# Mixture-of-experts layer on one core: from one 64-row expert block per pass to two blocks per pass, one in each column group of TensorE

## Chip, core and metric

One NeuronCore of a Trainium2 chip runs the whole layer in float32. The time is the device time of one execution in microseconds; the median of a few executions is given. The compute engines are PE (TensorE), DVE (VectorE), ACT (ScalarE), POOL (GpSimd) and SP (SyncE, which only issues DMAs here); 16 DMA engines move data.

## What is computed

A layer over 512 latent tokens of width 1024 with 256 context tokens: a projection, differential attention with four heads beside a pooling group, an output projection, and then a mixture of 64 SwiGLU experts (8 per token) with one shared expert. All that the change touches is the mixture:

```python
scores = jax.nn.sigmoid(t @ w_router)            # 512 x 64, top 8 per token in 4 of 8 groups
...
def expert_block(args):
    tok, wb, e = args
    xb = t_pad[tok]
    yb = swiglu(xb, w_e_gate[e], w_e_up[e], w_e_down[e])   # 1024 -> 256 -> 1024
    return yb * wb[:, None]
...
routed = jax.ops.segment_sum(yb.reshape(P, d), slot_tok, num_segments=T + 1)[:T]
shared = swiglu(t, w_sh_gate, w_sh_up, w_sh_down)
```

Every expert's weights are 3 MB (gate, up and down of 1 MB each), 201 MB in all, and each is read once. The 4096 pairs of token and expert are sorted by expert and cut into blocks of 64 slots; an expert with no full block has one part-filled block, and each has at least one.

## The kernel before

The first half (projections, attention, output projection, up to about 330 us) is not touched, but for where its results are kept. Each engine runs its own program, written out by hand, and they meet at semaphores.

**Routing and slot table (330 to 390 us).** DVE finds each token's eight experts, and from ranks (`ranks`, PE) the block and the place of every selected pair. The table of slots (which token and weight stands in each place of each block) is a product of one-hot matrices: `onehots(c)` on DVE makes the block one-hots (128 blocks wide, once with the token number, once with the weight), `pick_rows(c)` on ACT makes the place one-hots with eight Abs and one Relu, and `slot_table(c)` on PE multiplies them, 256 columns wide, for four chunks of 128 tokens. `quarters` (PE) spreads token numbers over partitions for the gather indices. Between these, PE does the shared expert (`shared_gate_up`, `shared_hidden`, `shared_down`), whose rows ACT stores to `sums[0]`. DVE writes `tab` (the expert of each block) and `ltab` (for each expert, the count of `s_dn` at which its last block is done).

**Weight stream (SP).** `wring` holds six experts. `load(n)` issues three 1 MB DMAs for expert n-1 (n = 0 is the shared expert). Before each, SP waits for `arrived(n-2)`, so that two are in flight, and then for `s_dn` to reach `ltab` of the expert whose slot is taken (lines 470 to 478, DMA issue at L432, arrival at L436).

**The expert loop.** A pass handles one block of 64 rows. PE's array is used as two column groups of 64 columns. Both work on the same block: group 0 takes the first half of the expert's columns straight from `wring`, group 1 the second half from a copy, `cur_g` (gate and up, made by DVE, two buffers, L1559) or `cur_d` (down, made by ACT, L761). Pass b on PE is: transpose of the hidden rows of block b-1 (`turn_hidden`, L1157), gate and up of block b (`gate_up`, L1141), down of block b-1 (`down`, L1150). The loop body is written for two passes (q = 0, 1) and the buffers alternate. In each pass:
- DVE (L1573 to L1582): waits for the next block's weights and copies half of gate and up; waits for the next block's gathered rows and transposes them (`turn_block`, L1563); multiplies silu, up and the slot weights (`hmid`, L1578); keeps the transposed hidden rows (L1582).
- ACT (L828 to L835): silu (L830), the index of a later gather (L765), the copy of half of the down weights (L761), then `keep_y`: when the scatter two passes back has landed, it copies the down product to `ysb` (L824), and the scatter's index (L768).
- POOL (L558, L559): two indirect gathers (L521) of 1 KB quarter rows of `h_rows` for block b+3, into `xg`, and one indirect scatter (L528) that adds 2 KB half rows to `sums[q]` in memory. Even and odd blocks add to different buffers, so two scatters may be in flight.

**Tail.** When all scatters have landed, SP and ACT load both sums, DVE adds and normalises them, and the output is stored; rows of the first two tiles are added to `out` by an accumulating DMA.

Of the kernel before, what the change touches and what calls it, by code (L numbers as in the profile page):

```python
# [23 lines left out]
P = 128  # L24
D = 1024
# [21 lines left out]
MAXB = 128  # L47
CW = KD * F
# [26 lines left out]
def constants():  # L75
# [16 lines left out]
    for a in range(NT):  # L92
        c[:, C_TOK + a] = 2 * (a * P + p) - FAR
    c[:, C_U] = p
    c[:, C_HALF] = FAR + p // SUB
    c[:, C_LO:C_LO + P] = (p % SUB + 1)[None]
# [7 lines left out]
    c[:, C_QUART] = 2 * FAR + p // 32  # L104
# [3 lines left out]
def build(nc, a, hbuf, sums, out):  # L108
    with ExitStack() as ctx:
# [14 lines left out]
        slot_idx = sb("slot_idx", [P, 136], I32)  # L124
        gidx = sb("gidx", [P, 2, 2], I32)
        sidx = sb("sidx", [P, 2], I32)
        slot_w = sb("slot_w", [P, 136])
        xg = sb("xg", [P, 2, D // 2])
# [13 lines left out]
        with ExitStack() as second:  # L142

            def sb2(name, shape, dt=F32):
                return second.enter_context(nc.sbuf_tensor(name, shape, dt))

            wring = sb2("wring", [P, NB * EW])
            cur_g = sb2("cur_g", [P, 2, 2, KD, P])
            cur_d = sb2("cur_d", [P, FJ, D // 2])
# [67 lines left out]
        nslo = kept[:, 832:864]  # L217
        pick = [heads[:, 3072 * i:3072 * i + 1024].rearrange("p (k q) -> p k q", k=TOPK) for i in range(2)]
        place2 = [heads[:, 3072 * i + 1024:3072 * i + 3072].rearrange("p (k v b) -> p k v b", k=TOPK, v=2)
# [3 lines left out]
        slot_g = cst[:, C_TRI:C_TRI + 2 * 136].bitcast(I32)  # L223
        vraw = rows[:, 1024:1024 + MAXB]
        xT = rows[:, 0:1024].rearrange("p (b k q) -> p b k q", b=2, k=KD)
        ysb = rows[:, 1024:2048].rearrange("p (b n) -> p b n", b=2)
        ysh = [hTt[i].rearrange("p k t -> p (k t)") for i in range(NT - 1)]
        ysh.append(cur_d[:].rearrange("p j n -> p (j n)"))
# [3 lines left out]
        sg = rows[:, 2048:2176]  # L232
        hmid = rows[:, 2304:2432]
        hTb = rows[:, 2560:2816].rearrange("p (b q) -> p b q", b=2)

# [96 lines left out]
        s_slo = sem("places_in_block")  # L332
        s_pick = sem("place_onehots")
# [13 lines left out]
        s_gt = [sem(f"gathered{i}") for i in range(2)]  # L347
        s_xte = sem("block_transposed")
# [9 lines left out]
        s_scat = [sem(f"scattered{i}") for i in range(2)]  # L358
# [6 lines left out]
        s_mixed = [sem(f"mixed_rows_stored{i}") for i in range(ADDED)]  # L365
# [18 lines left out]
        def _(sp):  # L384
# [33 lines left out]
            def load(n):  # L418
                if n == 0:
                    srcs = (a["w_sh_gate"][0].rearrange("(p k) f -> p (k f)", k=KD),  # L420
                            a["w_sh_up"][0].rearrange("(p k) f -> p (k f)", k=KD),
                            a["w_sh_down"][0].rearrange("(j p) n -> p j n", j=FJ))
                else:
                    srcs = (a["w_e_gate"][0, n - 1].rearrange("(p k) f -> p (k f)", k=KD),
                            a["w_e_up"][0, n - 1].rearrange("(p k) f -> p (k f)", k=KD),
                            a["w_e_down"][0, n - 1].rearrange("(j p) n -> p j n", j=FJ))
                for s, src in enumerate(srcs):
                    o = (n % NB) * EW + s * CW
                    dst = wring[:, o:o + CW]
                    if s == 2:  # L430
                        dst = dst.rearrange("p (j n) -> p j n", j=FJ)
                    sp.dma_start(dst, src).then_inc(s_wl[n % NB], 16)  # L432
# [6 lines left out]
            sp.dma_start(sums[1].rearrange("(p r) (h n) -> p (r h) n", p=P, h=2),  # L439
# [8 lines left out]
            for t in range(NT):  # L448
                if t < ADDED:
                    sp.wait_ge(s_x1, t + 1)  # L450
                    sp.dma_start(out[0, t * P:(t + 1) * P, :], xres[:, t, :]).then_inc(s_mixed[t], 16)
# [18 lines left out]
            for n in range(NB, NE):  # L470
# [3 lines left out]
                else:  # L474
                    if n == NB + 1:
                        sp.wait_ge(s_tab, 1)
                    sp.wait_ge(s_dn, sp.value_load(ltab[0:1, n - NB - 1:n - NB], min_val=NT + 2, max_val=MAXB + NT + 1))
                load(n)
            for n in range(NE - 2, NE):
                arrived(n)  # L480

            sp.wait_ge(s_routed, 1)
            for t in range(NT):
                sp.dma_start(acc[:, 0, t, :], sums[0][t * P:(t + 1) * P, :]).then_inc(s_yin[t][0], 16)
# [7 lines left out]
        def _(pool):  # L492
# [22 lines left out]
            srows = [x.rearrange("t (h n) -> (t h) n", h=2) for x in sums]  # L515

            def gather(b, q, set_by):
                pool.wait_ge(s_gi, set_by)
                pool.sem_inc(s_pgo, 1)
                for s in range(2):  # L520
# [1109 lines left out]
```

## Time and profile before

| | before |
|---|---|
| median of 3 runs | 1053.07 us (1050.58 to 1053.62) |
| profiled execution | 1052.63 us |
| its span | 1050.8 us |
| mean granted TensorE clock | 0.976 |
| PE busy | 963.3 us (92%) |
| DVE busy | 544.2 us (52%) |
| ACT busy | 377.6 us (36%) |
| POOL busy | 507.8 us (48%) |
| DMA | 296.18 MB, mean 282 GB/s |

The span runs from the first to the last instruction of the profiled execution, the time beside it is that of the same execution seen from outside. A busy share is a mean over stages with different limits. The page of the profile has the busy times, the span in 40 slices, the queues, the chain of work that ended last, and the costliest groups of instructions; views of the trace give the same for a stretch, an engine or a line. A float32 matmul stands in the trace as two records. Row costs on the DMA queues are told here as engine-us per MB: the share of the 16 engines, times the length of the stretch, times 16, by the MB moved. q1 is SP's queue, q10 ACT's and q0 POOL's.

### The profile page before, as it was taken

How to read it: one execution, taken by the hardware profiler on the slowest of the kernel's cores; microseconds unless marked ns; L12 is line 12 of the kernel's file. 1: busy time of each engine (PE TensorE's matmuls, PEld its weight loads, DVE VectorE, ACT ScalarE, POOL GpSimd, SP SyncE). 2: the span in 40 equal slices, each digit the busy share in tenths (PEclk: the TensorE clock that was granted, in tenths of full speed). 3: DMA queues.
4: the chain of work that ended last, by engine and by line, in shares of the span. 5: the costliest groups of instructions: out<-in, count | busy, mean ns of one | idle time of the engine just before them, and what ended most of it. 6: DMA issues, size and time to landing. Idle time of an engine off the chain costs nothing.

```text
span 1050.8 us, 19751 instructions
## 1 busy us (share of the span) xinstructions
PE 963.3 (92%) x5619; PEld 507.9 (48%) x5620; DVE 544.2 (52%) x833; ACT 377.6 (36%) x822; POOL 507.8 (48%) x351
## 2 busy tenths in 40 slices
PE   3999999899999998989999987999899999999970
PEld 0554444466555554545555444555455555555530
DVE  2336786777166834544555353455355545545434
ACT  4212222377245442323333333333233433333322
POOL 0312431000000025857777665777577777777751
PEclk9999999999999999999999999999999999999995
DMA  9955452800011958999998999999999999999917
GB/s 369 345 177 200 166 209 85 332 2 1 1 80 63 415 211 314 391 393 382 364 362 284 398 396 377 376 368 353 377 375 358 363 365 307 389 374 357 333 23 240
DMA packets 78313, 296.18 MB, mean 282 GB/s; under 512 B 18421, under 2 KB 19137, under 8 KB 58577
## 3 DMA queue, kind: packets, MB, share of 16 engines
q1 hardware_dynamic: 49874, 255.92, 62.1%
q0 software_dynamic: 26416, 35.70, 14.8%
q10 hardware_dynamic: 2000, 4.28, 1.0%
q8 instruction: 11, 0.18, 0.1%
q14 instruction: 12, 0.10, 0.0%
HBM read 280.83 MB, written 37.49 MB: 303 GB/s over the span
## 4 chain that ended last, share of the span: by engine, by line
PE 49%; DMA 36%; issue 5%; DVE 3%; SPq 2%; POOL 2%; ACT 2%; POOLq 0%; ACTq 0%; DVEq 0%
DMA wring<-in_w_e_down 29%; PE psum L905 13%; PE psum L1141 11%; PE psum L1150 5%; DMA xg<-h_rows,gidx 3%; PE psum L995 3%; PE psum L1107 3%; PE psum L975 3%; PE psum L942 3%; PE psum L966 2%; DMA ring<-in_w_ada 2%; POOL xg L521 1%; SPq L432 1%; DMA expert_sums<-rows,sidx 1%; PE psum L1084 1%
## 5 line engine op out<-in xcount | busy, mean ns | idle before, releaser
L1141 PE MATMUL psum<-wring,rows 128*64 x1664 | 389.3, 388 | 0.6
L1141 PE MATMUL psum<-cur_g,rows 128*64 128x256 f32 x1664 | 389.5, 389 | 0.0
L521 POOL DMA_INDIRECT xg<-h_rows,gidx x214 | 275.5, 1287 | 177.6 <-issue 106.8
L1141 PEld LDWEIGHTS psum<-wring,rows 128*64 128x64 f32 x1664 | 223.2, 139 | 122.8 <-issue 12.4
L1141 PEld LDWEIGHTS psum<-cur_g,rows 128*64 128x64 f32 x1664 | 223.6, 139 | 0.0
L1559 DVE COPY cur_g<-wring 128x2048 f32 x105 | 131.1, 1248 | 148.7 <-issue 75.3
L1150 PE MATMUL psum<-wring,rows 128*64 x420 | 197.5, 593 | 4.4 <-ACT cur_d L761 2.3
L528 POOL DMA_INDIRECT expert_sums<-rows,sidx x107 | 177.9, 1663 | 43.0 <-issue 32.1
L1150 PE MATMUL psum<-cur_d,rows 128*64 128x512 f32 x420 | 197.5, 593 | 0.0
L1563 DVE STREAM_TRANSPOSE rows<-xg 128x512 f32<-128x512 f32 x105 | 116.3, 1108 | 65.1 <-DMA xg<-h_rows,gidx 64.9
L761 ACT COPY cur_d<-wring 128x1024 f32 x104 | 108.9, 1047 | 99.1 <-PE psum L1150 88.5
L905 PE MATMUL psum<-actT,ring 128*128 128x512 f32 (+1 forms) x256 | 98.1, 547 | 1.3 <-DVE actT L1250 1.3
L830 ACT ACTIVATE rows<-psum 128x128 f32<-128x128 f32 x104 | 28.8, 277 | 192.0 <-PE psum L1141 192.0
L1150 PEld LDWEIGHTS psum<-wring,rows 128*64 128x64 f32 x420 | 57.4, 137 | 79.4 <-issue 64.7
L537 POOL TENSOR_TENSOR heads<-heads 128x512 f32<-128x512 f32 x4 | 5.1, 1270 | 162.0 <-DVE heads L1377 162.0
L1582 DVE COPY rows<-psum 128x128 f32<-128x128 f32 x104 | 30.4, 292 | 93.5 <-PE psum L1157 91.1
L510 POOL TENSOR_TENSOR ring<-ring 128x2048 f32<-128x2048 f32 x8 | 36.4, 4556 | 77.4 <-ACT ring L628 77.4
L905 PEld LDWEIGHTS psum<-actT,ring 128*128 128x128 f32 x256 | 49.8, 195 | 49.0 <-issue 46.9
L1157 PEld LDWEIGHTS psum<-cst,rows 128*128 128x128 f32 x105 | 14.7, 140 | 113.9 <-DVE rows L1578 112.3
L824 ACT COPY rows<-psum 128x512 f32<-128x512 f32 x105 | 61.1, 582 | 23.0 <-DMA expert_sums<-rows,sidx 19.9
L1157 PE MATMUL psum<-cst,rows 128*128 128x128 f32 x105 | 34.9, 333 | 27.7 <-DVE rows L1578 27.4
L1150 PEld LDWEIGHTS psum<-cur_d,rows 128*64 128x64 f32 x420 | 57.5, 137 | 0.0
(227 smaller groups left out, 937.0 us busy)
## 6 DMA issues: line engine op xcount, KB each, us to landing
wring<-in_w_e_gate SPq DMA_DIRECT2D x64, 1024.0 KB, 8.8
wring<-in_w_e_up SPq DMA_DIRECT2D x64, 1024.0 KB, 12.0
wring<-in_w_e_down SPq DMA_DIRECT2D x64, 1024.0 KB, 18.4
ring<-in_w_ada SPq DMA_DIRECT2D x20, 1024.0 KB, 4.9
ring<-in_w_in SPq DMA_DIRECT2D x4, 2048.0 KB, 29.2
heads<-in_w_ada SPq DMA_DIRECT2D x4, 1024.0 KB, 23.1
ring<-in_w_out SPq DMA_DIRECT2D x1, 4096.0 KB, 15.2
xg<-h_rows,gidx POOLq DMA_INDIRECT x214
```

Source lines behind the costliest of these rows:

```text
L510: pool.tensor_tensor(part[:, 2048:], part[:, 2048:], wrow[1], ALU.add).then_inc(s_part[1], 1)
L521: pool.indirect_dma_start(xg[:, q, 256 * s:256 * s + 256], None, hrows, bass.IndirectOffsetOnAxis(gidx[:, q, s:s + 1].bitcast(U32), 0), bo ...
L528: pool.indirect_dma_start(srows[q], bass.IndirectOffsetOnAxis(sidx[:, q:q + 1].bitcast(U32), 0), ysb[:, q, :], None, bounds_check=2 * T - ...
L761: act.copy(cur_d[:], w[:, :, D // 2:]).then_inc(s_cdn, 1)
L824: act.copy(ysb[:, q, :], pp[0][:, 512 * q:512 * q + 512]).then_inc(s_yev, 1)
L905: last = pe.matmul(o, l, r, start=(k == 0), stop=(k == KD - 1))
L942: last = pe.matmul(psum[:, o0:o0 + n], qT[64 * s:64 * s + 64, h, t * P:(t + 1) * P], kT[64 * s:64 * s + 64, h, c0:c0 + n], start=True, sto ...
L1141: last = pe.matmul(pp[2][SUB * g:SUB * g + SUB, 512 * q:512 * q + 2 * P] .rearrange("p (u f) -> p u f", u=2), xT[:, q, k, :], cur_g[:, q, ...
L1150: last = pe.matmul(pp[0][SUB * g:SUB * g + SUB, 512 * q:512 * q + 512], hTb[:, q, SUB * j:SUB * j + SUB], cur_d[:, j, :] if g else wring[: ...
L1157: pe.transpose(pp[3][:, 512 * q:512 * q + P], hmid, ident).then_inc(s_ht, 1)
L1559: dve.tensor_copy(cur_g[:, q], w[:, :, :, P:]).then_inc(s_cgu, 1)
L1563: dve.transpose(xT[:, q].rearrange("p k (s r) -> p s k r", s=2), xg[:, q, :].rearrange("p (s r k) -> p s k r", s=2, k=KD)).then_inc(s_xte, 1)
```

## The change

- A pass handles a pair of blocks, 2p and 2p+1. Column group 0 takes the first with all 256 (1024) columns of its expert from `wring`; group 1 the second with all columns of its expert from `cur_g` and `cur_d`, which now hold a whole expert each, in one buffer. `tab` is read for both blocks.
- `cur_g` is copied in two parts (3 and 5 of the 8 k), after the pair before has finished its gate and up; DVE's order in a pass becomes transpose, hidden product, copy, hidden rows. `cur_d` is copied in two parts (j).
- A gather fetches the pair's 128 rows with four indirect DMAs of 1 KB quarter rows, for pair p+2; a scatter adds 128 whole rows of 4 KB. Both halves add into one tensor of 1024 rows (group 0 into the first 512, group 1 into the others); each scatter's rows are kept only after the scatter before it has landed.
- `ltab` counts pairs.
- `w_e_down` is read with rows 2p and 2p+1 on partition p, 8 KB in one piece, and the hidden columns are transposed with a step of 2 to fit.
- The slot table is 128 places by 64 pairs; DVE makes the place one-hots with one compare, and `pick_rows` on ACT is gone.
- The buffers move: `xT` and `ysb` into `xres`, whose rows are therefore stored to `out` for all four tiles and the last two read back (`x1b`) at the end.

```diff
+PAIRS = MAXB // 2
+FIRST_KS = 3
...
-    c[:, C_HALF] = FAR + p // SUB
-    c[:, C_LO:C_LO + P] = (p % SUB + 1)[None]
+    c[:, C_HALF] = FAR + p // SUB * T
+    c[:, C_LO:C_LO + P] = (p + 1)[None]
...
-                            a["w_e_down"][0, n - 1].rearrange("(j p) n -> p j n", j=FJ))
+                            a["w_e_down"][0, n - 1].rearrange("(p j) n -> p (j n)", j=FJ))
...
+            sp.wait_ge(s_dn, sp.value_load(ltab[0:1, NE - NB - 1:NE - NB], min_val=NT + 2, max_val=PAIRS + NT + 1))
+            for t in range(ADDED, NT):
+                sp.wait_ge(s_mixed[t], 16)
+                sp.dma_start(x1b[:, t, :], out[0, t * P:(t + 1) * P, :]).then_inc(s_x1b, 16)
...
-            with pool.Fori(0, nb, 2) as i:
+            pairs = pool.snap((nb + 1) // 2)
+            with pool.Fori(0, pairs, 2) as i:
                 for q in range(2):
-                    gather(i + (q + 3), 1 - q, i + (q + 3))
-                    scatter(i + (q - 1), 1 - q)
+                    gather(i + (q + 2), q, i + (q + 2))
+                    scatter(i + (q - 1), 1 - q, ysb[:, 1 - q], i + (q + 2))
...
             def copy_down(e, w0):
                 act.wait_ge(s_w, e + 2)
-                w = wring[:, bass.ds(w0, CW)].rearrange("p (j n) -> p j n", j=FJ)
-                act.wait_ge(s_sh_st[NT - 1], 16)
-                act.copy(cur_d[:], w[:, :, D // 2:]).then_inc(s_cdn, 1)
+                for j in range(FJ):
+                    act.copy(cur_d[:, j, :], wring[:, bass.ds(w0 + j * D, D)]).then_inc(s_cdn, 1)
...
             def keep_y(n, q, scattered):
                 act.wait_ge(s_dn, n)
-                act.wait_ge(s_scat[q], scattered)
-                act.copy(ysb[:, q, :], pp[0][:, 512 * q:512 * q + 512]).then_inc(s_yev, 1)
-
-            with act.Fori(0, nb, 2) as i:
+                act.wait_ge(s_scat, scattered)
+                act.copy(ysb[:, q], pp[q]).then_inc(s_yev, 1)
+
+            with act.Fori(0, pairs, 2) as i:
                 for q in range(2):
+                    gather_index(i + (q + 2), q)
                     e, w0 = down_weights(i + q)
                     act.wait_ge(s_gu, i + (q + NT + 1))
-                    act.activation(sg, pp[2][:, 512 * q:512 * q + P], ACT.Silu).then_inc(s_sil, 1)
-                    gather_index(i + (q + 3), 1 - q)
+                    act.activation(sg, pp[2][:, 512 * q:512 * q + F], ACT.Silu).then_inc(s_sil, 1)
                     act.wait_ge(s_dn, i + (q + NT + 1))
                     copy_down(e, w0)
-                    keep_y(i + (q + NT + 1), 1 - q, i * 8 + 16)
+                    keep_y(i + (q + NT + 1), 1 - q, i * 16 + (16 * q + 16))
                     scatter_index(i + (q - 1), 1 - q)
...
-            def gate_up(q, w0):
+            def gate_up(p, q, w0):
                 w = wring[:, bass.ds(w0, 2 * CW)].rearrange("p (u k f) -> p u k f", u=2, k=KD)
+                pe.wait_ge(s_cgu, p * 2 + 1)
                 for k in range(KD):
+                    if k == FIRST_KS:
+                        pe.wait_ge(s_cgu, p * 2 + 2)
                     for g in range(2):
-                        last = pe.matmul(pp[2][SUB * g:SUB * g + SUB, 512 * q:512 * q + 2 * P]
+                        last = pe.matmul(pp[2][SUB * g:SUB * g + SUB, 512 * q:512 * q + 2 * F]
                                          .rearrange("p (u f) -> p u f", u=2),
-                                         xT[:, q, k, :], cur_g[:, q, :, k, :] if g else w[:, :, k, 0:P],
+                                         xT[:, q, k, SUB * g:SUB * g + SUB], cur_g[:, :, k, :] if g else w[:, :, k, :],
                                          start=(k == 0), stop=(k == KD - 1))
                 last.then_inc(s_gu, 1)
...
-            def down(q, w0):
+            def down(copied, q, w0):
                 for j in range(FJ):
-                    for g in range(2):
-                        last = pe.matmul(pp[0][SUB * g:SUB * g + SUB, 512 * q:512 * q + 512],
-                                         hTb[:, q, SUB * j:SUB * j + SUB],
-                                         cur_d[:, j, :] if g else wring[:, bass.ds(w0 + (2 * CW + j * D), 512)],
-                                         start=(j == 0), stop=(j == FJ - 1))
+                    pe.wait_ge(s_cdn, copied + j)
+                    for m in range(2):
+                        for g in range(2):
+                            last = pe.matmul(pp[q][SUB * g:SUB * g + SUB, 512 * m:512 * m + 512],
+                                             hTb[:, j, SUB * g:SUB * g + SUB],
+                                             cur_d[:, j, 512 * m:512 * m + 512] if g else
+                                             wring[:, bass.ds(w0 + (2 * CW + j * D + 512 * m), 512)],
+                                             start=(j == 0), stop=(j == FJ - 1))
                 last.then_inc(s_dn, 1)
...
-                then(dve.tensor_tensor(b[:, :, 1, :], row(C_IOTA, MAXB), col(sblk, MAXB), ALU.is_equal))
+                dve.tensor_tensor(pick[c % 2], row(C_LO, P), col(slo, P), ALU.is_equal)
+                then(dve.tensor_tensor(b[:, :, 1, :], row(C_IOTA, PAIRS), col(sblk, PAIRS), ALU.is_equal))
...
-            with dve.Fori(0, nb, 2) as i:
+            pairs = dve.snap((nb + 1) // 2)
+            with dve.Fori(0, pairs, 2) as i:
                 for q in range(2):
                     e, w0 = gate_up_weights(i + (q + 1))
-                    dve.wait_ge(s_gu, i + (q + NT))
-                    copy_gate_up(e, w0, 1 - q)
-                    turn_block(1 - q, i * 16 + 32 * (q + 1))
+                    turn_block(1 - q, i * 32 + 64 * (q + 1))
                     dve.wait_ge(s_sil, i + (q + NT + 1))
                     dve.scalar_tensor_tensor(hmid, sg, slot_w[:, bass.ds(i + q, 1)],
-                                             pp[2][:, 512 * q + P:512 * q + 2 * P], ALU.mult, ALU.mult)\
+                                             pp[2][:, 512 * q + F:512 * q + 2 * F], ALU.mult, ALU.mult)\
                        .then_inc(s_hm, 1)
+                    dve.wait_ge(s_gu, i + (q + NT + 1))
+                    copy_gate_up(e, w0)
                     dve.wait_ge(s_ht, i + (q + NT + 2))
-                    dve.tensor_copy(hTb[:, q, :], pp[3][:, 512 * q:512 * q + P]).then_inc(s_hte, 1)
+                    dve.wait_ge(s_dn, i + (q + NT + 1))
+                    dve.tensor_copy(hTb, pp[3][:, 512 * q:512 * q + F].rearrange("p (j q) -> p j q", j=FJ))\
+                       .then_inc(s_hte, 1)
```

## Rows read from the trace of the kernel before

**Rows 1.** The page: items of the chain that ended last; costliest group.
```profile
DMA wring<-in_w_e_down 29%; PE psum L905 13%; PE psum L1141 11%; PE psum L1150 5%; DMA xg<-h_rows,gidx 3%; PE psum L995 3%; PE psum L1107 3%; PE psum L975 3%; PE psum L942 3%; PE psum L966 2%; DMA ring<-in_w_ada 2%; POOL xg L521 1%; SPq L432 1%; DMA expert_sums<-rows,sidx 1%; PE psum L1084 1%
...
L1141 PE MATMUL psum<-wring,rows 128*64 x1664 | 389.3, 388 | 0.6
```

**Rows 2.** Busy time by stretch: PE, PEld, DVE, ACT, POOL, granted clock, DMA share, GB/s.
```profile
525.00:550.00 25.00, 25.00 (x190) 13.51 (x192) 13.05 (x18) 10.25 (x23) 19.57 (x14) 1.00 1.04 365
550.00:575.00 25.00, 25.00 (x183) 12.69 (x177) 13.10 (x18) 8.93 (x22) 18.88 (x14) 1.00 0.87 273
```

**Rows 3.** SyncE's waits, 460 to 1000 us: releaser: us in total, times, longest.
```profile
SPq L436 <- DMA wring<-in_w_e_down: 413.0, 51, 9.9
SPq L432 <- PE psum L1150: 20.9, 4, 8.8
```

**Rows 4.** DMA queues, 460 to 1000 us: packets, MB, share of 16 engines.
```profile
q1 hardware_dynamic: 29363, 164.70, 76.6%
q0 software_dynamic: 22034, 31.14, 24.6%
```

**Rows 5.** Chain in order of time: start us, us, what.
```profile
480.25 3.67 PE psum L1141 x32
...
558.44 3.60 PE psum L1141 x32
562.04 1.72 PE psum L1150 x8
563.76 0.26 PE psum L1157
...
772.09 9.25 DMA expert_sums<-rows,sidx
...
810.05 8.18 DMA xg<-h_rows,gidx
```

**Rows 6.** SyncE in order of time: loads 7, 22, 43 and 54 begin.
```profile
409.59 0.34 SPq L432 DMA_DIRECT2D wring<-in_w_e_gate  x1
...
563.80 0.33 SPq L432 DMA_DIRECT2D wring<-in_w_e_gate  x1
...
760.41 0.33 SPq L432 DMA_DIRECT2D wring<-in_w_e_gate  x1
...
882.15 0.33 SPq L432 DMA_DIRECT2D wring<-in_w_e_gate  x1
```

**Rows 7.** DMA queue q1, 3 to 22 us (w_ada, rows of 8 KB).
```profile
q1 hardware_dynamic: 1408, 7.71, 99.5%
```

**Rows 8.** DMA queue q1, 199 to 203 us (w_out, rows of 4 KB).
```profile
q1 hardware_dynamic: 222, 1.58, 99.1%
```

**Rows 9.** DMA queue q0, 1042 to 1050 us (accumulating stores, rows of 4 KB).
```profile
q0 software_dynamic: 195, 0.67, 46.6%
```

**Rows 10.** The page: groups of instructions, busy us, mean ns, idle before.
```profile
L521 POOL DMA_INDIRECT xg<-h_rows,gidx x214 | 275.5, 1287 | 177.6 <-issue 106.8
...
L528 POOL DMA_INDIRECT expert_sums<-rows,sidx x107 | 177.9, 1663 | 43.0 <-issue 32.1
...
L761 ACT COPY cur_d<-wring 128x1024 f32 x104 | 108.9, 1047 | 99.1 <-PE psum L1150 88.5
```

**Rows 11.** Scatters (tile expert_sums): time from issue to landing.
```profile
DMA to landing us min/median/max: 3.5/8.5/19.6
```

**Rows 12.** PE in order of time, slot table chunks 2 and 3.
```profile
369.56 7.49 PE L1084 MATMUL psum<-heads 128*128 128x256 f32 x32 [1.03 <-ACT heads L750]
```

**Rows 13.** DVE in order of time: the last useful copy of gate and up weights.
```profile
1002.91 1.23 DVE L1559 COPY cur_g<-wring 128x2048 f32 x1 [6.31 <-SPq L436]
```

**Rows 14.** Chain in order of time, last passes.
```profile
1005.78 5.36 PE psum L1141 x32
...
1020.81 1.96 PE psum L1150 x8
```

**Rows 15.** DMA queue q0, 550 to 575 us.
```profile
q0 software_dynamic: 1134, 1.30, 32.3%
```

More of the change, by code:

```diff
@@ L357, in build @@
         s_yev = sem("down_evacuated")
-        s_scat = [sem(f"scattered{i}") for i in range(2)]
+        s_scat = sem("scattered")
         s_routed = sem("all_scattered")
@@ L364, in build @@
         s_last = sem("last_tile_stored")
-        s_mixed = [sem(f"mixed_rows_stored{i}") for i in range(ADDED)]
+        s_mixed = [sem(f"mixed_rows_stored{i}") for i in range(NT)]
         s_frs = sem("final_rms")
@@ L546, in _ @@
             pool.wait_ge(s_clr, 1)
-            for q in range(2):
-                gather(q, q, 1)
+            gather(0, 0, 1)
+            pool.wait_ge(s_sh_st[0], 16)
+            gather(1, 1, 1)
             pool.wait_ge(s_sum0, 16)
-            for q in range(2):
-                scatter(-1, q, True)
-            gather(2, 0, 2)
+            pool.wait_ge(s_adre, 8)
+            scatter(-2, 0, arow[:, 3], 1)
             for t in range(NT):
@@ L570, in _ @@
                 pool.dma_start(out[0, t * P:(t + 1) * P, :], acc[:, 0, t, :], accum_op=ALU.add).then_inc(s_out, 16)
-            n_g0 = pool.snap(pairs * 32 + 64)
-            n_g1 = pool.snap(pairs * 32 + 32)
-            pool.wait_ge(s_gt[0], n_g0)
-            pool.wait_ge(s_gt[1], n_g1)
+            n_gathered = pool.snap(turns * 64 + 64)
+            for q in range(2):
+                pool.wait_ge(s_gt[q], n_gathered)
         @block.scalar
@@ L1091, in quarters @@
                 pe.wait_ge(s_raw, 1)
-                for s in range(2):
+                for s in range(4):
                     for c in range(4):
-                        last = pe.matmul(pp[2][32 * c:32 * c + 32, MAXB * s:MAXB * s + MAXB],
-                                         cst[:, C_ID + 32 * s:C_ID + 32 * s + 32], vraw, start=True, stop=True)
+                        last = pe.matmul(pp[2][32 * c:32 * c + 32, PAIRS * s:PAIRS * s + PAIRS],
+                                         cst[:, C_ID + 32 * s:C_ID + 32 * s + 32], vraw[:, 0:PAIRS],
+                                         start=True, stop=True)
                 last.then_inc(s_sel2, 1)
@@ L1154, in down @@
                 last.then_inc(s_dn, 1)
             def turn_hidden(q):
-                pe.transpose(pp[3][:, 512 * q:512 * q + P], hmid, ident).then_inc(s_ht, 1)
+                for j in range(FJ):
+                    last = pe.transpose(pp[3][:, 512 * q + j * P:512 * q + (j + 1) * P], hmid[:, j:F:FJ], ident)
+                last.then_inc(s_ht, 1)
             shared_gate_up(0, range(KD))
@@ L1186, in _ @@
             nb = pe.value_load(ntab[0:1, 0:1], min_val=E, max_val=MAXB - 1)
+            pairs = pe.snap((nb + 1) // 2)
             pe.wait_ge(s_yev, NT - 1)
-            with pe.Fori(0, nb, 2) as i:
+            with pe.Fori(0, pairs, 2) as i:
                 for q in range(2):
@@ L1595, in finish @@
                     then(last)
-                    last = dve.tensor_tensor(y, y, xres[:, t, :], ALU.add)
+                    dve.wait_ge(s_x1b, 16 * (NT - ADDED))
+                    last = dve.tensor_tensor(y, y, x1b[:, t, :], ALU.add)
                 last.then_inc(s_fin, 1)
```

237 lines of the change are left out of this document (110 added, 127 removed).

## Prediction

> **What bounds the kernel now.** Read the chain of work that ended last first [rows 1]: after the dense front half, its largest single item is the landing of `w_e_down`, the last third of an expert's weights. Next the table by stretches [rows 2]: while the experts run, the 16 DMA engines are busy 1.04 of the time and TensorE is busy too; only between 550 and 575 us does the DMA share fall (0.87). The DMA queue's own waits [rows 3] decide between the two: from 460 to 1000 us SyncE waited 413.0 us in 51 waits for weights to arrive (it keeps two experts in flight), but only 20.9 us in 4 waits for TensorE to give a ring slot back. So the loop is a weight stream that is nearly always full, and the places where it runs dry are those four waits. [rows 4] split its time: 76.6% of 16 engines for 164.70 MB of weights (40.2 engine-us per MB), 24.6% for 31.14 MB of gathered and scattered rows (68 per MB).
>
> TensorE has two regimes. In the stretch of many-block experts it is the bound: a pass is 3.60 + 1.72 + 0.26 = 5.58 us [rows 5]. In stretches of one-block experts it waits for weights. There are 104 passes (1664 matmul records at L1141 on each column group [rows 1], 16 in each pass). The reference's router, applied to its inputs, gives 103 blocks of 64; experts 0 to 9 have one each, 10 to 16 have 2, 1, 2, 4, 3, 5, 1, and 40 to 47 have 4, 3, 2, 1, 2, 2, 1, 5. The two long releases in the SyncE queue [rows 6] fit this: load 22 (expert 21) is issued at 563.80, when expert 15 (five blocks, the ring has 6 slots) is done; load 54 at 882.15, when expert 47 is.
>
> **Pass of a pair.** There are 52 passes of two blocks. Four down records of 512 columns per column group take 1.72 us, 0.43 each, the two groups at once [rows 5]. Gate and up are now 16 records of 256 columns, half of that each, 3.44, and 0.16 of start to make 3.60; after, 16 records of 512 columns: 6.88 + 0.16 = 7.0. Down: 8 x 0.43 = 3.4. Two transposes for one: 0.26 + 0.1. Sum 10.8 us, against 11.16 for two passes now. TensorE gains 0.36 us per pair, some 19 us in all, but this counts only where TensorE is the bound.
>
> **The ring, where the change costs.** A block's weights are given back when its down product is done, one pass after its gate-up. Now that is 11.2 us after the block starts; after, 21.6 us, and an expert whose last block shares a pair with the next expert waits for the pair. Blocks 0 to 26 belong to experts 0 to 15, so expert 15 ends in pair 13, beside expert 16, and is released at the end of pass 14.
> - Start: load 7 now goes at 409.59 [rows 6]. After, expert 0 is released by pass 1 at about 414: pass 0 can start at 393 (the slot table is earlier, below), pass 1's gate-up begins at 404 after `cur_g` is free, and its down ends at 414. Loads 7 and 8 then go together, where now load 8 waits for a later pass than load 7, so the stream is only about 2 us late.
> - First gap: the chain has expert 12's first pass at 480.25 [rows 5]. After, pair 6 (experts 11, 12) starts at about 481, and passes 6 to 14 are 9 x 10.8 = 97.2, so load 22 goes at 578.2 instead of 563.80: +14.4 us, the 2 of the start included. The weights of the other ring slots are long in place, so the DMA engines stand idle, and the stream that follows is a full one: the delay stays.
> - Next 20 loads, to expert 40: each is cheaper by the DMA terms below, 0.15 us: -3.
> - Second stretch: now from the arrival of expert 40 (load 43 is issued on it, 760.41) to 882.15 is 121.8 us for 21 passes, since gathers and scatters are in the chain there (the last two of rows 5). After: 1.2 us for the first part of the copy, then passes 30 to 40, 11 x 10.8 = 118.8: 120.0, -1.8. Expert 47 ends with block 79, exactly a pair, so nothing is lost by sharing.
> - Last 11 loads: -1.6, but expert 48's slot comes 10.8 us after expert 47's, not 5.6, and an expert takes about 9 to load: +1.5.
> Together the last weights arrive 14.4 - 3 - 1.8 - 0.1 = 9.5 us later.
>
> **DMA terms.** Bytes stay the same; rows are larger. `w_e_down` is read in 8 KB rows, not 4 KB: rows of 8 KB cost 0.995 x 19 x 16 / 7.71 = 39.2 engine-us per MB [rows 7], rows of 4 KB 0.991 x 4 x 16 / 1.58 = 40.1 [rows 8]. 1.05 MB x 0.9 / 16 = 0.06 us per expert. Scatters move 4 KB rows, not 2 KB halves: of the 68 per MB, gathers (half the bytes, plain reads) should take about 40 like the weights, which leaves 96 for accumulating scatters. An accumulating store of 4 KB rows stands at the end of the trace: 0.466 x 8 x 16 / 0.67 = 89 [rows 9]. 0.26 MB per expert x 7 / 16 = 0.11 us. Sum 0.17, taken as 0.15. Bounds: 0 (the same per byte) to the price of a plain copy (40 for the scatter: 0.9 us per expert). I take 89, because it is the same operation with the same row. The Trainium skill (DMA: Bandwidth & Descriptors, "Why small descriptors are slow (HBM only)") gives each packet a fixed 3 cycles beside its 32-byte beats; by it the scatter would gain 3/134, 2%, an estimate from that page of about 2 us in all; the rows show 7%, and the measurement is what I use.
>
> **Gathers and scatters.** The gathers are the same in number, scatters are half. POOL has 4 x 1.29 + 1.66 = 6.8 us per pair [rows 10], in a pass of 10.8: not a bound. But all scatters now add into one buffer, so ACT keeps pair j's rows only after pair j-1's scatter has landed. One link is landing + a copy of 128x1024, 1.05 [rows 10], + 0.5 for index and issue. A scatter lands 8.5 us after issue (median) [rows 11], 9.25 in the chain [rows 5]. Same number of packets per engine but each with twice the bytes: +1.2; but no longer right behind two gathers in its queue: -1 to -2. That is 8.5 + 1.5 = 10 to 9.4 + 1.2 + 1.5 = 12.1, against 10.8. I take it as just hidden, and keep 12 for the range. Behind this wait on ACT stand the next gather's index and the next silu. The last of a pair's four gathers is issued about 10 us into a pass, lands 8.2 us later [rows 5] and is turned by DVE ahead of the hidden product and the copy that the next pass waits for, with under 1 us to spare. The Trainium skill (same page, "Anatomy of one DMA — SWDGE (gpsimd) path") puts such a DMA at 2 us plus its bytes at 436 GB/s; for 512 KB that is an estimate of 3.2 us, and the chain of scatters would never count. The landings of this trace disagree with it under the weight stream.
>
> **Slot table.** ACT's eight Abs and a Relu go; VectorE does one more 1.2 us compare, on a table half as wide; TensorE's 32 matmul records that take 7.49 us for two of the four chunks [rows 12] become half as wide: the table is done some 6 us earlier, the first pass 3 us earlier (four gathers and a double transpose take the rest). It ends in idle DMA time, since load 7 waits for the release at 414 anyway: 0. The 1 MB of x rows stored and read back, and the extra constants, lie where DMA is idle: 0; if not, 3 us.
>
> **Tail.** Now: the last copy begins at 1002.91, the last down starts at 1020.81 and ends at 1022.8, 20 us after the arrival [rows 13, 14], with DVE's copy, transpose and hidden product and the work of two blocks in the chain. After: 1.3 for the copy, 7.0 + 1.8 (the gate-up behind the idle time takes 5.36 instead of 3.6 [rows 5, 14], as now) + 3.4 + 1.0 + 3.4 = 17.9: -2.1. But the last rows can be kept only when the scatter before them has landed: its index is set 3.4 us after the down before the last, it lands 3.5 later, while the last down ends after 4.4, so +3 with the keep of twice the columns. Net +0.9.
>
> **Sum.** Profiled execution 1052.63 (span 1050.8 and 1.8 around it) + 9.5 + 0.9 = 1063.0. The median of the runs is 1053.07, 0.4 more, within their spread. Forecast 1063.
>
> **Rivals.**
> (a) The serial scatters, or the gather behind them, set the pass of full pairs: 12.0 instead of 10.8. About 6 full pairs in the first stretch and 5 in the second, 11 x 1.2 = 13: 1076. For: landings of 8.5 to 9.3. Against: in such a stretch the weight stream dries up, and the landings shorten.
> (b) The accumulating scatter of whole rows is much cheaper than 89. This takes the DMA time off 31 streamed loads and the kernel becomes faster. To cancel +10.4 it needs 0.34 us per load, or 0.34 x 16 / 0.26 = 21 less: it decides at 68 engine-us per MB. At 60 it would be 29 x 0.26 / 16 = 0.47 per load, x 31 = 14.6 off: 1048. Against: [rows 9] is the same operation. For: that row is a short sample with few packets.
> (c) The later release costs little, because load 22 overlaps with row traffic piled up before it (its share is still 32.3% of the engines from 550 to 575 [rows 15]) and the pass is a bit shorter: about +3 at the first gap instead of +14, which gives 1063 - 11.4 = 1051.6: no change.
>
> **Chances.** A measurement of this kernel tells some 0.3%, 3.2 us, from no change. Forecast (1056.5 to 1069) 0.45, (a) 0.2, (b) 0.2, (c) 0.15. So faster 0.2, same 0.15, slower 0.65. The range takes in (c), the near part of (b) and (a): 1046 to 1077.
>
> **What would show it.** Passes 10.8 us apart in the many-block stretches; load 22 near 578 and more DMA idle before it than now; SyncE's waits for slots over 40 us instead of 20.9; the q0 queue's cost per MB near 64; last weights at 1008 to 1013. ACT's wait for the scatter before it tells (a): passes of 12. If q0's cost is under 56 per MB, (b) holds. The forecast is wrong if the stream is not what the end waits for.

## The result, and the profile after

The changed kernel takes 1082.17 us (median of 4 runs, 1078.99 to 1084.97), the one before 1053.34 in the same session (4 runs). The ratio is 1.0278, 95% interval [1.0243, 1.0313]: slower by 2.8%. The forecast was 1063.0 with a range to 1077: the sign was right, but two thirds of the loss were not foreseen. The profiled execution took 1083.2 us, its span is 1081.4, 30.6 more than before.

The page of the changed kernel, its chain that ended last and four groups of instructions (columns as in rows 10):
```profile
DMA 42%; PE 40%; issue 7%; DVE 4%; ACTq 2%; ACT 2%; POOL 1%; SPq 1%; POOLq 1%; DVEq 0%
...
L1128 PE MATMUL psum<-wring,xres 128*64 x832 | 380.6, 612 | 58.0 <-DVE cur_g L1552 51.1
L1556 DVE STREAM_TRANSPOSE xres<-xg 128x1024 f32<-128x1024 f32 x53 | 108.3, 2043 | 271.0 <-DMA xg<-h_rows,gidx 270.6
L529 POOL DMA_INDIRECT expert_sums<-xres,sidx x53 | 88.3, 1667 | 245.7 <-ACT sidx L752 125.4
L806 ACT COPY xres<-psum 128x1024 f32<-128x1024 f32 x53 | 53.5, 1010 | 104.8 <-DMA expert_sums<-xres,sidx 104.8
```
TensorE does what it did in fewer, wider records, but it now stands idle for 58 us ahead of its gate-up products (0.6 in rows 1). ScalarE, in line 806 (the copy that keeps a pair's rows), waits 104.8 us for the scatter before.

The chain in order of time, 938 to 1010 us: start, length, what:
```profile
941.06 10.24 DMA expert_sums<-xres,sidx
...
952.57 0.51 issue
953.30 10.28 DMA expert_sums<-xres,sidx
...
965.59 10.26 DMA expert_sums<-xres,sidx
...
977.85 10.04 DMA expert_sums<-xres,sidx
```
Scatter follows scatter, 12.0 to 12.3 us apart. These landings are 27% of the chain (1% in rows 1), those of `w_e_down` 9% (29%). The step from one landing to the next issue can be seen on ScalarE (start, length, line, operation, idle time before it and its releaser):
```profile
951.33 1.01 ACT L806 COPY xres<-psum 128x1024 f32<-128x1024 f32 x1 [2.88 <-DMA expert_sums<-xres,sidx]
952.24 0.19 ACT L752 COPY sidx<-slot_idx 128x1 int32 x1
952.33 0.20 ACT L749 COPY gidx<-cst 128x4 int32 x1
954.10 0.38 ACT L813 ACTIVATE rows<-psum 128x256 f32<-128x256 f32 x1 [1.57 <-PE psum L1128]
```
Landing 10.26, copy 1.01, index and issue 1.0: one link is 12.2 us. Behind it in ScalarE's program stands the index of the next gather (L749), as the prediction said.

SyncE's waits, 460 to 1000 us (beside rows 3), and the DMA queues, 460 to 1030 us (beside rows 4):
```profile
SPq L435 <- DMA wring<-in_w_e_down: 281.6, 42, 9.0
SPq L431 <- PE psum L1139: 107.4, 17, 29.2
```
```profile
q1 hardware_dynamic: 23025, 167.61, 72.6%
q0 software_dynamic: 15506, 30.95, 22.4%
```
The wait for ring slots (L431, released by TensorE) has grown from 20.9 to 107.4 us. The price of bytes fell a little: weights 0.726 x 570 x 16 / 167.61 = 39.5 engine-us per MB (40.2 before), rows 0.224 x 570 x 16 / 30.95 = 66 (68 before).

Stretches (columns as in rows 2; the next to last is the share of the DMA engines):
```profile
400.00:425.00 25.00, 22.67 (x108) 7.66 (x106) 10.37 (x10) 6.94 (x12) 13.76 (x12) 1.00 0.32 113
550.00:575.00 25.00, 23.78 (x112) 8.22 (x110) 13.01 (x13) 7.54 (x13) 14.89 (x12) 1.00 0.72 221
575.00:600.00 25.00, 22.69 (x106) 7.76 (x104) 10.13 (x10) 6.94 (x12) 15.32 (x13) 1.00 0.69 219
825.00:850.00 25.00, 23.36 (x110) 8.07 (x108) 10.05 (x10) 8.18 (x15) 15.68 (x12) 1.00 0.76 254
900.00:925.00 25.00, 22.97 (x106) 7.96 (x106) 12.39 (x14) 8.46 (x14) 16.11 (x13) 1.00 0.78 243
```
The weight stream stands still for part of the time at the start (DMA share 0.32) and in both stretches of many-block experts (0.69 to 0.78). Loads 7, 22, 54 and 64 as SyncE issues them (beside rows 6; load 64 was at 982.91 before):
```profile
417.49 0.34 SPq L431 DMA_DIRECT2D wring<-in_w_e_gate  x1
...
588.07 0.33 SPq L431 DMA_DIRECT2D wring<-in_w_e_gate  x1
...
912.47 0.33 SPq L431 DMA_DIRECT2D wring<-in_w_e_gate  x1
...
1007.59 0.33 SPq L431 DMA_DIRECT2D wring<-in_w_e_gate  x1
```
They are 7.9, 24.3, 30.3 and 24.7 us later than before. Of the 30.6 us, 24.7 are in the stream and 5.9 in the tail behind it.

Times of single events can be compared between two traces only with care: the half of the kernel ahead of the experts does not end at the same moment in each profiled execution. Its last operation on GpSimd (L537) starts at 350.71 us before and at 350.80 in the changed kernel, but earlier in some of the runs below, as here in the kernel before with late slots:
```profile
347.45 1.27 POOL L537 TENSOR_TENSOR heads<-heads 128x512 f32<-128x512 f32 x1 [6.00 <-DVE heads L1377]
```
Where such a difference is over half a microsecond it is taken off below, and "aligned" says so.

### The profile page after: what moved, and what is told of

The parts are those of the page before. It is cut to its first block, busy times and chain, and to the rows that moved or that the text cites. A ratio compares the mean times of both kernels' runs of the same rounds, so it can differ in the third digit from the quotient of the medians.

```text
span 1081.4 us, 13440 instructions
## 1 busy us (share of the span) xinstructions
PE 948.7 (88%) x3980; PEld 391.6 (36%) x3981; DVE 512.2 (47%) x684; ACT 328.1 (30%) x577; POOL 411.2 (38%) x300
## 3 DMA queue, kind: packets, MB, share of 16 engines
q0 software_dynamic: 18880, 35.68, 13.9%
## 4 chain that ended last, share of the span: by engine, by line
DMA 42%; PE 40%; issue 7%; DVE 4%; ACTq 2%; ACT 2%; POOL 1%; SPq 1%; POOLq 1%; DVEq 0%
DMA expert_sums<-xres,sidx 27%; PE psum L889 13%; DMA wring<-in_w_e_down 9%; PE psum L1128 7%; PE psum L1139 3%; DMA xg<-h_rows,gidx 3%; PE psum L979 3%; PE psum L926 3%; PE psum L959 3%; PE psum L950 2%; PE psum L1091 2%; DMA ring<-in_w_ada 2%; POOL xg L522 1%; ACTq L739 1%; PE psum L844 1%
## 5 line engine op out<-in xcount | busy, mean ns | idle before, releaser
L1128 PE MATMUL psum<-wring,xres 128*64 x832 | 380.6, 612 | 58.0 <-DVE cur_g L1552 51.1
L1128 PE MATMUL psum<-cur_g,xres 128*64 128x512 f32 x832 | 380.8, 612 | 0.0
L1556 DVE STREAM_TRANSPOSE xres<-xg 128x1024 f32<-128x1024 f32 x53 | 108.3, 2043 | 271.0 <-DMA xg<-h_rows,gidx 270.6
L1128 PEld LDWEIGHTS psum<-wring,xres 128*64 128x64 f32 x832 | 112.7, 141 | 281.9 <-issue 280.2
L1139 PE MATMUL psum<-wring,rows 128*64 x424 | 190.6, 592 | 1.7 <-ACT rows L745 1.7
L1139 PE MATMUL psum<-rows 128*64 128x512 f32 x424 | 190.6, 592 | 0.0
L745 ACT COPY rows<-wring 128x1024 f32 x104 | 103.6, 1044 | 170.1 <-PE psum L1139 150.5
L1552 DVE COPY cur_g<-wring 128x1536 f32 x106 | 127.3, 1242 | 51.1 <-SPq L435 47.1
L1128 PEld LDWEIGHTS psum<-cur_g,xres 128*64 128x64 f32 x832 | 112.6, 141 | 0.0
L1139 PEld LDWEIGHTS psum<-wring,rows 128*64 128x64 f32 x424 | 58.0, 137 | 121.1 <-issue 121.1
L806 ACT COPY xres<-psum 128x1024 f32<-128x1024 f32 x53 | 53.5, 1010 | 104.8 <-DMA expert_sums<-xres,sidx 104.8
L1573 DVE SCALAR_TENSOR_TENSOR rows<-rows,slot_w,psum 128x256 f32<-128x256 f32 x52 | 23.6, 453 | 62.9 <-ACT rows L813 57.7
```

The lines of the kernel that those rows point to most:

```text
L745: act.copy(cur_d[:, j, :], wring[:, bass.ds(w0 + j * D, D)]).then_inc(s_cdn, 1)
L806: act.copy(ysb[:, q], pp[q]).then_inc(s_yev, 1)
L1128: last = pe.matmul(pp[2][SUB * g:SUB * g + SUB, 512 * q:512 * q + 2 * F] .rearrange("p (u f) -> p u f", u=2), xT[:, q, k, SUB * g:SUB * g ...
L1139: last = pe.matmul(pp[q][SUB * g:SUB * g + SUB, 512 * m:512 * m + 512], hTb[:, j, SUB * g:SUB * g + SUB], cur_d[:, j, 512 * m:512 * m + 51 ...
L1552: dve.tensor_copy(cur_g[:, :, k0:k1, :], w[:, :, k0:k1, :]).then_inc(s_cgu, 1)
L1556: dve.transpose(xT[:, q].rearrange("p k (s r) -> p s k r", s=4), xg[q].rearrange("p (s r k) -> p s k r", s=4, k=KD)).then_inc(s_xte, 1)
```

## The experiments

There are two theories. **Ring:** slots are given back one pass of a pair later, so the weight stream stops. **Serial scatters:** the link of 12.2 us sets the pass instead of TensorE's 10.8. Both delay the release of slots, so the wait for slots alone can't tell them apart. All ratios are to the kernel before, on the same chip. "By the ratios" means a difference of two ratios times 1053 us.

**Move the scatter's wait from ScalarE to GpSimd** (in the changed kernel; copies are made early, only the issue waits; a semaphore for each parity):
```
-                act.wait_ge(s_scat, scattered)
+                act.wait_ge(s_scat[q], scattered)
...
+                    pool.wait_ge(s_scat[q], i * 8 + (16 * q + 16))
                     scatter(i + (q - 1), 1 - q, ysb[:, 1 - q], i + (q + 2))
```


> The changed kernel, but the wait for the scatter before moves from ACT (ahead of keeping the rows) to POOL (ahead of issuing the scatter); ACT waits only for the scatter two passes back, whose buffer it reuses. Theory S (one link of serial scatters, landing 10.3 + keep and index 2.0 = 12.3 us, sets the pass): the link falls to landing + 0.5 = 10.8, about TensorE's own pass, so 1.4 us less on some 28 links, and the stream of weights takes over in part: 1055 to 1065. Theory R (the ring slots given back later are the cost, the scatters only look late): no change beyond 3 us, 1079 to 1085.

Measured 1078.54 us, ratio 1.0243 [1.0204, 1.0282]: some 4 us less than the changed kernel, with intervals that overlap, and next to the ring theory's figure. The pass in the first many-block stretch (from one silu to the next, mean of pairs 6 to 14) fell from 11.62 to 11.10 us. Load 22 came at 580.54, 7.5 us sooner, but 3.5 of these were there before the experts began; aligned it is 4.1, eight passes of 0.5.

**No serial wait at all:** scatters of odd pairs go to another tensor, which is left out of the result, and ScalarE waits only for the scatter two pairs back.
```
-                pool.indirect_dma_start(sums, bass
+                pool.indirect_dma_start(sums_odd if q else sums, bass
```


> The changed kernel, but odd pairs scatter into a tensor of their own, so that no scatter waits for the one before; this tensor is not added to the output, so the odd pairs' share is left out of the result (and 4 MB more are zeroed near 200 us, where DMA is idle). Theory S: passes of 10.8 in the many-block stretches, and what is left over 1053 is the ring and the tail: 1056 to 1063, near the forecast of 1063 less 3 for the tail. Theory R: 1075 or more.

Measured 1073.79 us, ratio 1.0187 [1.0142, 1.0232]: just under the ring theory's 1075, far from the other's 1056 to 1063. Most passes of the many-block stretch are 10.88 us apart, as the prediction worked out for TensorE (11.02 in the mean of pairs 6 to 14), and SyncE's waits, 430 to 1030 us, are
```profile
SPq L435 <- DMA wring<-in_w_e_down: 376.1, 52, 10.2
SPq L431 <- PE psum L1146: 111.1, 15, 28.0
```
The wait for slots has not shrunk (111.7 in the changed kernel in this stretch). Cutting the chain of scatters alone brings back, by the ratios, 9.6 of 29 us.

**The kernel before, slots given back two passes (11.2 us) later:**
```
-                then(dve.tensor_scalar(ltab[0:1, :], cum[0:1, :], float(NT + 1), None, ALU.add))
+                then(dve.tensor_scalar(ltab[0:1, :], cum[0:1, :], float(NT + 3), None, ALU.add))
```


> The kernel before, with every ring slot given back two passes (11.2 us) later than its expert is done, and nothing else. By the ring step of the prediction (a slot held about 10 us longer leaves the DMA engines idle at expert 15 and a little at the start and at expert 47): 1063 to 1073, load 22 near 575. If the ring has slack for that: 1050 to 1057.

Measured 1075.63 us, ratio 1.0224 [1.0178, 1.0269]. Nothing but the release differs, and it costs 2.2%, more than the 1063 to 1073 that the ring step of the prediction gave. SyncE's waits, 430 to 1030 us:
```profile
SPq L436 <- DMA wring<-in_w_e_down: 400.0, 55, 9.8
SPq L432 <- PE psum L1150: 86.4, 23, 22.0
```
Load 7 goes at 417.49 and load 22 at 583.43. This execution was 3.3 us ahead when the experts began, so aligned they are 11.2 and 22.9 us later than before: the delay of 11.2 is paid at the start, and once more in the first gap. From load 43 to load 54, the second gap, it is paid a third time (132.7 us for 121.7). Elsewhere part comes back: loads 22 to 43 take 4.3 us less and loads 54 to 64 3.5 less.

**The same with half of the delay** (`float(NT + 2)`, one pass of 5.6 us later):

> The kernel before, each ring slot given back one pass (5.58 us) later instead of two, as in e3_before_late_release (which came to 21 to 23 us for 11.2 us of delay). If each stretch of many-block experts pays its delay in full (start, first gap, second gap), it is half of that: 1062 to 1066. If the ring has slack for a first delay and pays from a threshold on: 1054 to 1059.

Measured 1062.12 us, ratio 1.0098 [1.0070, 1.0126]. Aligned (1.9 us), load 7 is 4.9 us late and load 22 10.6, again the delay twice. By the ratios 10.3 us for 5.6 of delay and 23.6 for 11.2: there is no slack that takes the first microseconds.

**Half of the scattered bytes** (in the changed kernel, rows of the second column group are put out of bounds):
```
-    c[:, C_HALF] = FAR + p // SUB * T
+    c[:, C_HALF] = FAR + p // SUB * 4 * T
```


> The changed kernel, but the rows of the second column group are not scattered (their indices are out of bounds), so half of the mixture's sum is left out; the serial wait stays. If a scatter's landing goes with its bytes, it falls from 10.2 to about 7.5 us, the link to 9.5, under TensorE's pass, and the time to 1050 to 1062. If the landing is mostly fixed (issue, queue, receipt under the weight stream), it stays over 9 and the time over 1070.

Measured 1073.74 us, ratio 1.0191 [1.0141, 1.0241]. Its chain in order of time:
```profile
496.66 10.31 DMA expert_sums<-xres,sidx
508.97 9.90 DMA expert_sums<-xres,sidx
520.88 9.69 DMA expert_sums<-xres,sidx
532.56 9.33 DMA expert_sums<-xres,sidx
```
With half of the bytes a scatter still lands in 9.3 to 10.3 us here: the landing goes with its bytes only a little. What fills it, the weights beside it or the gathers behind it in GpSimd's queue, no run separates. From 480 to 1000 us the row queue has 22.03 MB at 16.2% of the engines against 29.12 MB at 23.0%: (0.230 - 0.162) x 520 x 16 / 7.09 = 80 engine-us for each MB that is gone, near the 89 that was taken for accumulating stores. Loads 22 to 43 take 191.3 us here, 190.7 in the changed kernel, so the bytes that are gone bring nothing there. What the kernel gains by the ratios, 9.2 us, is elsewhere: the passes of pairs 6 to 14 take 11.35 us in the mean, load 22 comes at 583.36, and the second gap (loads 43 to 54) takes 129.8 instead of 133.7.

**Slots back early.** The two blocks of a pair change column groups (in the changed kernel). The earlier block then works from the copies, the later one from the ring, and an expert whose last block is the earlier of its pair frees its slot with the copy (`downs` is one less for it, `copied` the count of copies made by then):
```
-                e = dve.value_load(tab[0:1, bass.ds(p * 2 + 3, 1)], min_val=0, max_val=E - 1)
+                e = dve.value_load(tab[0:1, bass.ds(p * 2 + 2, 1)], min_val=0, max_val=E - 1)
...
-                    sp.wait_ge(s_dn, sp.value_load(ltab[0:1, n - NB - 1:n - NB], min_val=NT + 2, max_val=PAIRS + NT + 1))
+                sp.wait_ge(s_dn, downs) 
+                sp.wait_ge(s_cdn, copied)
```


> The changed kernel with the two blocks of a pair in the other column group: the earlier block now has the group that works from copies, the later block the group that reads the ring. With it SyncE may give a slot back when the copies of its expert's last block are made, if that block is the earlier of its pair (for the others, when the pair's down product is done, as before). A slot such as that of expert 0 or of expert 15 (the wait before load 22) then comes free some 9 us sooner (one pass of 10.9 less the 2.0 of the copy). Order, count and size of all products, scatters and gathers stay; ScalarE's serial wait for the scatter before it stays. Ring theory (slots given back late are the larger cost): load 7 at 408 to 410 instead of 417.5, load 22 at 571 to 579 instead of 588.1, time 1062 to 1072. Rival, serial scatters (the pass of 11.6 to 12.2 is what counts, the release adds little): 1077 to 1083.

Measured 1076.62 us, ratio 1.0224 [1.0204, 1.0245]: between the two forecasts and next to the rival's, though load 7 did come at 409.56 and load 22 at 572.12, 8 and 16 us sooner, as the ring theory said. Of these 16 us only 9 are left at load 64. The chain of work that ended last, the first two and the last of its 17 scatters from 629 to 837 us:
```profile
629.78 9.28 DMA expert_sums<-xres,sidx
641.07 10.94 DMA expert_sums<-xres,sidx
...
826.91 10.17 DMA expert_sums<-xres,sidx
```
Passes are 12.3 us apart here (from 629.78 to 826.91, 16 links): with slots in time, the scatters set the pace, also where one-block experts stream.

**Early slots and the wait on GpSimd together:**

> Both: the early release of e5_early_copies and the wait for the scatter before on GpSimd, as in e1_pool_waits (which alone took 4 us off). Ring theory with the scatter's share on top: 1057 to 1067, passes of 10.9 to 11.1 in the many-block stretches, SyncE's waits for slots under 70 us. If it is no faster than e5_early_copies, the serial wait costs nothing once slots come early. Rival, serial scatters as the main cost: 1073 to 1079, as e1_pool_waits.

Measured 1060.07 us, ratio 1.0076 [1.0056, 1.0095]. The page's chain and SyncE's wait for slots, 430 to 1030 us:
```profile
DMA wring<-in_w_e_down 37%; PE psum L902 13%; PE psum L1141 8%; DMA expert_sums<-xres,sidx 4%; PE psum L1152 4%; PE psum L992 3%; PE psum L972 3%; PE psum L939 3%; PE psum L963 2%; PE psum L1104 2%; SPq L432 2%; DMA ring<-in_w_ada 2%; DMA x
```
```profile
SPq L432 <- PE psum L1152: 20.2, 5, 8.8
```
The weight stream heads the chain again. By the ratios, early slots alone gave 5.7 us, the moved wait alone 3.7 (within the noise), the two together 21.3: each had been hidden behind the other. The change of column groups, which comes with the early slots, was not run by itself; what it does without them isn't known. A link is now 11.2 us, a landing of 10.2 plus 1.0, for the copy is made beside it (GpSimd in order of time, scatters alone):
```profile
500.16 1.62 POOL L536 DMA_INDIRECT expert_sums<-xres,sidx  x1 [2.98 <-DMA expert_sums<-xres,sidx]
...
511.35 1.62 POOL L536 DMA_INDIRECT expert_sums<-xres,sidx  x1 [3.77 <-DMA expert_sums<-xres,sidx]
```

**Early slots and two targets:**

> The early release of e5_early_copies with the two scatter targets of e2_two_targets: the scatters of odd pairs add into a tensor of their own, which is not added to the result (it lacks the mixture rows of the odd pairs), so no scatter waits for the one before it. If the serial scatters still cost something once their wait stands on GpSimd (gathers queued behind it), this comes under e6_early_copies_pool_waits (1060.1): 1050 to 1057. If what is left of the loss is only the coarser grain of the pass (a slot comes back 9 to 21 us after its block starts, not 11, and the second many-block stretch ends some 6 us later than before), it is the same as e6_early_copies_pool_waits: 1057 to 1062.

Measured 1056.27 us, ratio 1.0023 [1.0003, 1.0043]. So the link of 11.2 us still cost 5.6 us by the ratios, and without both causes the change is nearly even, 2.4 us above the kernel before. This kernel leaves the odd pairs out of its result; a version to keep would still have to add the second pair of sums.

**One part alone in the kernel before: place one-hots on VectorE.**
```
-                    last = act.activation(pick[c % 2][:, k, :], cst[:, C_LO:C_LO + P], ACT.Abs,
-                                          bias=nslo[:, c * TOPK + k:c * TOPK + k + 1], scale=1.0)
...
+                dve.tensor_tensor(pick[c % 2], row(C_LO, P), col(nslo, P), ALU.is_equal)
```


> The kernel before with one part of the change alone: the 128x1024 table of place one-hots is one compare of 1.2 us on VectorE for each chunk of tokens, in place of eight Abs and a Relu on ScalarE (3.6 us a chunk). The table of slots keeps its width. By the prediction's step (the earlier table ends in time in which the stream waits for a slot anyway): 1052 to 1054.5. Rival (load 7 waits for block 0, and block 0 for the table, so that the whole stream moves by what the table gains, 2 to 5 us): 1048 to 1051.

Measured 1054.58 us, ratio 1.0010 [0.9994, 1.0027]: no difference. Load 5, which waits for the table, goes at 384.89 (383.96 before), aligned 2.6 us later: VectorE, with four compares more and a table of full width, doesn't make the table earlier. Load 22 is then 2.4 us later (aligned, one execution each). So the run doesn't test whether an earlier table is worth nothing; it rather speaks for a stream that moves with the table. In the changed kernel load 5 goes at 376.98; its table has half the width, and this is probably what makes it early, but that was not run alone. None of these kernels is faster than the one before.

## Why the prediction was wrong

**Bound of the kernel, and the order of terms: right.** The stream of weights, the few waits for slots and both many-block stretches were where the time went.

**Start, "only about 2 us late": wrong.** Load 7 was forecast at 414 and went at 417.49, since the first gate-up, behind idle time, took 9.83 and not 7.0 us (the prediction allowed for that in the tail only, and with 1.8). And it looked no further than load 8: load 9 waits for the next pair, 430.77 instead of 422.89. The start is 7.9 us late. The two runs of the kernel before with late slots show that a delay at the start is not absorbed by load 22.

**First gap, "load 22 goes at 578.2": it went at 588.07.** The silu of pair 6 is at 491.71, which puts its start at 484.6 and not 481, 3.6 us; eight passes of 11.62 instead of 10.8 are 6.6. These are the 10 us that were missed. The release itself, a pass of a pair later, was sized right.

**Next loads, -3:** loads 22 to 43 took 190.7 us instead of 196.6, -5.9. The kernel before with slots two passes late, old rows and all, has 192.3, so some 4.3 of it may come with the gap and not with the change of rows (why wasn't tested), and 1.6 would be left for the cheaper rows.

**Second stretch, "120.0": 133.7.** Ten passes of 11.6 for 10.8 (silu of pair 30 at 793.09, of pair 40 at 909.04) are 8.0; and pair 30 doesn't start with its weights, since TensorE still has pair 29: its silu comes 14.4 us after load 43, where 1.2 + 7.2 was counted, 5.9. Together 13.9. The arrival of an expert was taken for the start of its pass in a stretch where the pass was already the slower of the two. With two targets, where the pass is close to 11, the stretch still takes 128.6 us, so this second part doesn't come from the scatters.

**Last ten loads, -0.1:** 95.1 instead of 100.8, -5.7; the kernel before with slots two passes late also gains 3.5 there (97.3).

**Pass "just hidden": the step that failed.** The prediction had 10 to 12.1 us for a link of scatters against a pass of 10.8 and took it "as just hidden"; the link is 12.2 (landing 10.26; copy, index and issue 2.0), and passes took 11.6. This is the largest single miss: 6.6 us in the first gap and 8.0 in the second. The link came out at the upper end of the prediction's own sum, and rival (a) was right that it sets the pass. Its size was not: (a) charged the longer pass only in 11 passes and came to 1076, but the chain of scatters also sets the pace of streaming stretches. The argument that landings shorten where the stream dries up holds for two passes out of nine: loads 17 to 21 still stream into the stretch (they are issued from 504 to 554 us), and only at its end is the wait gone, as ScalarE's rows show:
```profile
558.86 1.01 ACT L806 COPY xres<-psum 128x1024 f32<-128x1024 f32 x1 [2.66 <-DMA expert_sums<-xres,sidx]
...
569.93 1.01 ACT L806 COPY xres<-psum 128x1024 f32<-128x1024 f32 x1 [1.67 <-DMA expert_sums<-xres,sidx]
...
579.31 1.00 ACT L806 COPY xres<-psum 128x1024 f32<-128x1024 f32 x1
```
The Trainium skill (DMA: Bandwidth & Descriptors, "Anatomy of one DMA — SWDGE (gpsimd) path") would have 3.2 us for the landing of a full scatter of 512 KB, an estimate from that page. This trace disagrees by a factor of three while weights stream (10.24 to 10.28 us), although a scatter carries some 0.34 MB only: twice the 7.09 MB that half of the rows made, over the 42 scatters of that stretch.

**Prices of bytes: right, and of no use.** 66 engine-us per MB for rows where 64 was forecast; weights 39.5. Rival (b) fell: accumulating stores cost 80 per MB, and it needed less than 68. Rival (c), that later slots cost little, fell with the two late-release runs.

**Tail, "+0.9": +5.9.** From load 64 to the end of the span 73.8 us, not 67.9. The chain there:
```profile
1020.49 7.79 DMA xg<-h_rows,gidx
...
1031.78 7.09 PE psum L1128 x32
1038.87 3.45 PE psum L1139 x16
...
1046.43 5.94 DMA expert_sums<-xres,sidx
...
1054.37 4.43 DMA expert_sums<-xres,sidx
```
The end waits for a gather, late because its index stands behind the scatter's wait on ScalarE, and then for two scatters in a row, 5.94 and 4.43, where one of 2.74 stood before. The prediction counted one such landing at 3.5; the 1.8 that it allowed for a gate-up behind idle time didn't come (7.09). With the wait moved to GpSimd alone, the gather is gone from this chain, but TensorE then stands idle before the gate-up, which takes 9.84 us, and the tail is 73.5 all the same. With early slots too it is 69.8, with early slots and two targets 66.5.

Sum of the stream: 24.3 - 5.9 + 11.9 - 5.6 = 24.7, forecast 14.4 - 3 - 1.8 - 0.1 = 9.5. In the terms of the experiments, of 29.3 us by the ratios 21.3 go to late slots and to the link's part on ScalarE together and can't be shared out, 5.6 to the rest of the link, and 2.4 are left. How these divide between the coarser pass and the tail stays open.

## What to carry to other kernels

When a transfer that used to have two buffers is made serial, take the link at its landing beside the full stream, with everything between landing and next issue, and compare it with the pass in every stretch, not only where the engine is the bound. When a buffer of a ring is given back later, count the delay once for every stretch in which the stream waits for a slot (here the start and two gaps), not once for the kernel: with the stream near full little absorbs it. Where two waits can each hide the other, take both away in one run before either is called harmless. And before an event's time is compared between two traces, look whether the part that wasn't touched ended at the same time in both.

## What the runs showed of the hardware that was not expected

An accumulating scatter of 128 row places (some 80 of them filled, 0.34 MB) lands in 10.2 us while weights stream, in 9.3 to 10.3 with half of the bytes, and at the end of the kernel, when no weights and no gathers move, in 5.94 us with 0.23 MB and in 4.43 with 0.04 MB. So even a scatter that carries next to nothing takes 4.4 us from issue to landing here, and traffic beside it adds several microseconds, where leaving out half of its bytes saved less than one. TensorE's first wide gate-up takes 9.83 us instead of 7.02, as the chain has it:
```profile
393.30 9.83 PE psum L1128 x32
...
407.00 7.02 PE psum L1128 x32
```
TensorE had been idle for 4.94 us before the first pair; from 393 to 398 us the granted clock is 0.50, the lower of its two levels (1.2 of 2.4 GHz), from 399 to 407 it is 1.00:
```profile
393.00:398.00 5.00, 4.70 (x12) 1.49 (x14) 0.09 (x1) 0.00 (x0) 0.78 (x1) 0.50 1.01 394
399.00:407.00 8.00, 8.00 (x40) 2.65 (x38) 3.70 (x4) 0.72 (x3) 4.92 (x4) 1.00 0.11 34
```
That is 2.8 us more, where the narrower pass before paid 1.8 (5.36 for 3.60, rows 14 and 5). In the changed kernel four more gate-ups begin with such slow records (1.1 us each), behind 9.32, 5.95, 7.63 and 5.34 us of idle time; the mean granted clock is 0.73, 0.52, 0.59 and 0.62 there (440 to 446, 458 to 464, 609 to 615 and 664 to 670 us). Those behind 1.5 to 3.6 us of idle time don't.
